# Values and output gates of the recurrent mixer, projected together from slab pairs

## What is computed

```python
proj = x @ w_in                                  # (512, 1024) @ (1024, 4096)
q, f, i, g = jnp.split(proj, 4, axis=-1)
k = (1.0 - lbf) * jax.nn.sigmoid(-ff);  q = jax.nn.silu(q);  v = i
...                                              # 8 heads of 128, chunks; state S_t = diag(f_t) S_{t-1} + k_t v_t^T
o = rms_norm(o, norm_g).reshape(B, S, HGRN_WIDTH) * jax.nn.silu(g)
return o.astype(x.dtype) @ w_out
```

## Time and profile before

| | us |
|---|---|
| median of 3 runs | 1959.66 (1959.48 to 1960.23) |
| the profiled execution | 1960.62 |
| its span, first to last instruction | 1958.9 |
| PE busy | 1933.7 (99% of the span) |
| POOL busy / DVE busy / ACT busy | 898.7 / 1103.5 / 631.9 |
| the recurrent mixer, first level products to last down product | 1320 to 1593, within the span |

### The profile page before, as it was taken

How to read it: one execution, slowest core, us unless ns; L and a number is a source line. 1 busy time by engine, 2 the same in 40 slices (tenths; PEclk the granted TensorE clock), 3 DMA queues, 4 the chain that set the end, 5 groups by cost and what they waited for, 6 DMA issues and landing times.

```text
span 1958.9 us, 26063 instructions
## 1 busy us (share of the span) xinstructions
PE 1933.7 (99%) x10793; PEld 1633.3 (83%) x10793; DVE 1103.5 (56%) x1552; ACT 631.9 (32%) x789; POOL 898.7 (46%) x596
## 2 busy tenths in 40 slices
PE   8999999999999999999999999999999999999997
PEld 8888888978779888888988888899988888888886
DVE  2755473566473765563465647365544675546555
ACT  3333232264433333322333323232233123323321
POOL 4454555543233555445445446454333345355544
PEclk9999999999999999999999999999999999999999
DMA  6232322321204233232423232322221213332321
GB/s 237 91 104 85 129 86 88 110 67 65 65 22 151 89 117 104 79 108 87 151 86 108 65 129 86 108 87 87 77 75 66 65 62 111 108 121 95 104 69 43
DMA packets 135589, 185.44 MB, mean 95 GB/s; under 512 B 3360, under 2 KB 119088, under 8 KB 135472
## 3 DMA queue, kind: packets, MB, share of 16 engines
q1 hardware_dynamic: 135312, 183.53, 28.3%
q10 hardware_dynamic: 160, 0.26, 0.1%
HBM read 181.42 MB, written 2.10 MB: 94 GB/s over the span
## 4 chain that ended last, share of the span: by engine, by line
PE 95%; DVE 3%; ACT 1%; DMA 1%; issue 0%; SPq 0%; POOL 0%; DVEq 0%; ACTq 0%
PE psum L1513 30%; PE psum L1514 29%; PE psum L1515 29%; PE psum L1823 2%; PE psum L1764 1%; PE psum L1537 1%; PE psum L1777 1%; PE psum L1796 1%; DMA raw<-in_ffn_w 1%; PE psum L1851 0%; DVE x L1112 0%; DVE arena L1223 0%; PE psum L1854 0%; PE psum L1841 0%; DVE arena L1222 0%
## 5 line engine op out<-in xcount | busy, mean ns | idle before, releaser
L693 POOL TENSOR_TENSOR w_lo<-raw,w_hi 128x512 fp32r<-128x512 f32 x524 | 848.7, 1653 | 933.1 <-ACT w_hi L756 908.6
L1513 PE MATMUL psum<-xt_hi,w_hi 128*128 128x512 f32 (+1 forms) x1824 | 675.6, 370 | 2.2 <-DVE w_lo L1383 0.9
L1514 PE MATMUL psum<-xt_lo,w_hi 128*128 128x512 f32 (+1 forms) x1824 | 670.7, 368 | 0.0
L1515 PE MATMUL psum<-xt_hi,w_lo 128*128 128x512 f32 (+1 forms) x1824 | 670.7, 368 | 0.0
L1513 PEld LDWEIGHTS psum<-xt_hi,w_hi 128*128 128x128 f32 x1824 | 343.8, 188 | 66.2 <-issue 5.5
L1515 PEld LDWEIGHTS psum<-xt_hi,w_lo 128*128 128x128 f32 x1824 | 343.9, 189 | 57.1
L1514 PEld LDWEIGHTS psum<-xt_lo,w_hi 128*128 128x128 f32 x1824 | 344.0, 189 | 55.5
L756 ACT ACTIVATE w_hi<-raw 128x2048 fp32r<-128x2048 f32 x132 | 251.8, 1911 | 341.9 <-PE psum L1515 340.0
L1072 DVE SCALAR_TENSOR_TENSOR x<-psum,x 128x512 f32<-128x512 f32 x224 | 145.4, 683 | 131.6 <-PE psum L1515 128.4
L770 ACT ACTIVATE gate<-psum 128x512 f32<-128x512 f32 x88 | 52.5, 598 | 308.9 <-PE psum L1515 308.9
L1112 DVE SCALAR_TENSOR_TENSOR x<-psum,x 128x512 f32<-128x512 f32 x124 | 83.0, 687 | 105.8 <-PE psum L1515 105.6
(11 more groups left out here) (181 smaller groups left out, 2163.1 us busy)
## 6 DMA issues: line engine op xcount, KB each, us to landing
raw<-in_ffn_w SPq DMA_DIRECT2D x115, 1024.0 KB, 5.4
raw_odd<-in_ffn_w SPq DMA_DIRECT2D x16, 1024.0 KB, 5.1
raw<-in_hgrn_w_in SPq DMA_DIRECT2D x16, 1024.0 KB, 5.4
raw<-in_attn_w_in SPq DMA_DIRECT2D x9, 1024.0 KB, 5.3
raw<-in_attn_w_out SPq DMA_DIRECT2D x4, 1024.0 KB, 5.4
raw<-in_hgrn_w_out SPq DMA_DIRECT2D x4, 1024.0 KB, 4.9
lng<-in_ln_g SPq DMA_DIRECT2D x6, 512.0 KB, 4.2
lnb<-in_ln_b SPq DMA_DIRECT2D x6, 512.0 KB, 5.2
```

Of the source, the lines that this page charges most:

```text
L693: op = pool.tensor_tensor(w_lo[:, slot_of[s], cols], raw[:, slot_of[s], cols], w_hi[:, slot_of[s], cols].bitcast(F32), ALU.subtract)
L1513: pe.matmul(out_, w[0], xs[0], start=first, stop=False)
L1514: pe.matmul(out_, w[0], xs[1], start=False, stop=False)
L1515: return pe.matmul(out_, w[1], xs[0], start=False, stop=last)
```

## The change

The v and g slabs of a group are replaced by a pair, `vg0` and `vg1`. Each holds 256 columns of v and the same 256 of g side by side (512 columns) for half of the contraction: `vg0` rows 0 to 511, `vg1` rows 512 to 1023. A quarter pair (two quarters, one block) now makes one token tile of both, 512 columns wide: its first quarter reads the slab `vg0`, its second the slab `vg1`. So both slabs of a pair are in use from the second quarter of `vg0` to the last of `vg1`.

```diff
-HGRN_PART = {"q": 0, "f": 1, "v": 2, "g": 3}
+HGRN_PART = {"q": 0, "f": 1}
+VG_HALF = {"vg0": 0, "vg1": 1}
...
-             [[("v", 0), ("g", 0), ("f", 1), ("q", 1), ("g", 1)], [("v", 1), ("down", 0), ("f", 2), ("q", 2), ("g", 2)],
-              [("v", 2), ("f", 3), ("q", 3), ("down", 1)], [("v", 3), ("g", 3), ("down", 2)]]),
+             [[("vg0", 0), ("vg1", 0), ("f", 1), ("q", 1), ("vg0", 1)],
+              [("vg1", 1), ("down", 0), ("f", 2), ("q", 2), ("vg0", 2)],
+              [("vg1", 2), ("f", 3), ("q", 3), ("down", 1)], [("vg0", 3), ("vg1", 3), ("down", 2)]]),
...
-        if step[0] == "quarter" and step[2] == 3:
+        if step[0] == "quarter" and step[2] == 3 and slabs[step[1]][0] != "vg0":
             near = [i for i in range(at + 1, min(at + 1 + reach, len(plan))) if plan[i][0] in urgent]
-            out.setdefault(near[0] if near else at, []).append(step[1] + RING)
+            freed = [step[1] - 1, step[1]] if slabs[step[1]][0] == "vg1" else [step[1]]
+            out.setdefault(near[0] if near else at, []).extend(s + RING for s in freed)
...
+            def load_vg(s, half, g):
+
+                sp.wait_ge(*raw_free[s])
+                dst = raw[:, slot_of[s], :].rearrange("p (c n) -> p c n", n=2 * GW)
+                rows = hw_in[0].rearrange("(c p) n -> p c n", p=P)[:, 4 * half:4 * half + 4, :]
+                for k in range(2):
+                    first = (2 + k) * D + g * GW
+                    sp.dma_start(dst[:, :, k * GW:(k + 1) * GW],
+                                 rows[:, :, first:first + GW]).then_inc(raw_landed[slot_of[s]], 16)
...
-                elif name == "g":
-                    op = act.activation(out_gate[:, g % 2, 2 * j:2 * j + 2, :], two_tiles, ACT.Silu)
                 else:
-                    op = act.activation(values[:, g % 2, 2 * j:2 * j + 2, :], two_tiles, ACT.Copy)
+                    t = 2 * VG_HALF[name] + j
+                    act.activation(values[:, g % 2, t, :], src[:, 0:GW], ACT.Copy)
+                    op = act.activation(out_gate[:, g % 2, t, :], src[:, GW:2 * GW], ACT.Silu)
...
+                first = s - VG_HALF.get(name, 0)
+                slot = slot_of[first + half] if name in VG_HALF else slot_of[s]
                 if quarter == 0:
                     pe.wait_ge(lo_ready, s + 1)
+                if name == "vg0" and quarter == 1:
+                    pe.wait_ge(lo_ready, s + 2)
...
+                if name in VG_HALF:
+                    t = 2 * VG_HALF[name] + j
+                    tok = slice(t * P, (t + 1) * P)
+                    for c in range(DC // 2):
+                        cols = slice(c * 2 * GW, (c + 1) * 2 * GW)
+                        c_ = half * DC // 2 + c
+                        mm = three(out_, (xt_hi[:, c_, tok], xt_lo[:, c_, tok]), (w_hi[:, slot, cols], w_lo[:, slot, cols]),
+                                   c_ == 0, c_ == DC - 1)
...
-            def outputs(g):
+            def outputs(g, blocks_needed):
+                pe.wait_ge(proj_kept, blocks_needed)
                 pe.wait_ge(states_ready, g + 1)
```

More of the change, by code:

```diff
@@ L169, in mixer_schedule, with splits @@
     return steps
-def splits(plan, urgent, reach):
+def splits(plan, slabs, urgent, reach):
     out = {}
     for at, step in enumerate(plan):
-        if step[0] == "quarter" and step[2] == 3:
+        if step[0] == "quarter" and step[2] == 3 and slabs[step[1]][0] != "vg0":
             near = [i for i in range(at + 1, min(at + 1 + reach, len(plan))) if plan[i][0] in urgent]
-            out.setdefault(near[0] if near else at, []).append(step[1] + RING)
+            freed = [step[1] - 1, step[1]] if slabs[step[1]][0] == "vg1" else [step[1]]
+            out.setdefault(near[0] if near else at, []).extend(s + RING for s in freed)
     return out
@@ L460, in build_trunk @@
                 raw_free[s], w_free[s] = last_raw.get(slot), last_w.get(slot)
-                n_loads[slot] += 1
+                n_loads[slot] += 2 if name is not None and name[0] in VG_HALF else 1
                 raw_loads[s] = 16 * n_loads[slot]
@@ L474, in build_trunk @@
                     blocks += 2
-                    last_w[slot] = proj_done, blocks
+                    last_w[slot] = proj_done, blocks + 2 * (name[0] == "vg0")
         def left_parts(name):
@@ L622, in _ @@
                             load_params(n)
+                        if name in VG_HALF:
+                            load_vg(s0 + s, VG_HALF[name], g)
+                            continue
                         if kind == "attn":
@@ L732, in _ @@
                     low(s0 + RING + 1)
-                    split_at = splits(plan, ("outputs",), 2)
+                    split_at = splits(plan, slabs, ("outputs",), 2)
                     for at, step in enumerate(plan):
@@ L967, in _ @@
                         high(s0 + s + RING)
-                    split_at = splits(plan, ("turn_out", "outputs"), 1)
+                    split_at = splits(plan, slabs, ("turn_out", "outputs"), 1)
                     for at, step in enumerate(plan):
@@ L1269, in norm_outputs @@
                 dve.wait_ge(rms_ready, g + 1)
-                dve.wait_ge(proj_kept, first_block + blocks_until("hgrn", "g", g))
+                dve.wait_ge(proj_kept, first_block + blocks_until("hgrn", "vg1", g))
                 dve.wait_ge(keys_tok_ready, 2 * g + 2)
@@ L1738, in projected @@
                 out_ = bank[j]
-                token_major = name in ("v", "g", "vb")
-                if not token_major:
+                if name in VG_HALF:
+                    t = 2 * VG_HALF[name] + j
[5 more added lines that the diff above has]
+                                   c_ == 0, c_ == DC - 1)
+                elif name != "vb":
                     for c in range(4 * half, 4 * half + 4):
@@ L1931, in _ @@
                         elif what == "updates":
-                            updates(g, first + blocks_until(kind, "v", g))
+                            updates(g, first + blocks_until(kind, "vg1", g) - 1)
                         elif what == "outputs":
-                            outputs(g)
+                            outputs(g, first + blocks_until(kind, "vg1", g))
                         elif what == "norm":
```

1 line of the change is left out of this document (removed).

## The result

The changed kernel takes **1965.09 us** (median of 8 executions, 1963.13 to 1967.9) against 1960.0 us for the kernel before (8 executions, 1959.48 to 1960.38): ratio 1.0028, 95% interval 1.0019 to 1.0036. It is slower by 5.1 us; 2.1 us were forecast, and the time lies at the upper edge of the range on record (1956.0 to 1965.2). A second set of 9 executions gave 1965.18 against 1959.93 (31 executions), the same ratio.

What follows compares the result with a forecast made beforehand. PE, busy 99% of the span, was taken to bound the kernel. Terms -4.05 - 0.4 + 0.3 + 2.15 + 3.2 + 0.9 = +2.1 us on a median of 1959.66 gave 1961.8 us, range 1956.0 to 1965.2.

Steps and rivals of the forecast that it cites:

- 8 quarters: v and g quarters of a group: 12 products of 512 columns instead of 24 of 256, 0.135 us gained each.
- level 7: Scaling ahead of this level held by back-to-back lows: +0.3 us in group 0, +3.2 us in group 2.
- level 5: Group 1: a second low in a row holds DVE's scaling, so PE waits for the add: +2.15 us.
- `low(19)` gone: Group 3: this low no longer runs between levels 6 and 7 and holds DVE's scaling: -0.4 us.
- ACT's wait: Group 3: the outputs' first product waits until ACT has kept the last vg1 block: +0.9 us.
- Group 2's walk: Ahead of group 2's level 7: four DVE instructions, each let in once per POOL piece, delay PE by 3.2 us.
- C: Rival: POOL keeps the port through a whole low, DVE gets in only at its end: +6.5 us, 1966.1; chance 0.08.
- D: Rival: PE's pace at 512 columns is no better with weights as the moving side: 1965.8 us; chance 0.04.
- A: Rival: held DVE instructions cost nothing, as PE has more slack than read: -3.6 us, 1956.1; chance 0.12.
- B: Rival: group 2's L1195 and L1197 pass freely beside a low, the rest holds: -0.4 us, 1959.3; chance 0.16.
- Part 4's cover: At the end: `low(19)` done at 1578.95, PE needs it at 1579.9; slack 0.9 us, so costed at nothing.
- part 1: v and g products: 30 of 32 quarters gain 0.135 us each from 512-column products, -4.05 us in all.

Runs made afterwards that it cites:

- apart_all: The changed kernel with slabs 6 and 15 split one slab later and slab 10 waiting for six of group 1's eight down blocks: 1956.44 us, ratio 0.9985.
- apart_g1: The changed kernel with only slab 10's split put off, waiting for six of the eight blocks of group 1's down slab: 1961.97 us, ratio 1.0012.
- again3: The changed kernel without an edit, profiled once more: 1965.91 us, mean granted clock 0.996.
- again2: The changed kernel without an edit, profiled once more: 1962.88 us, mean granted clock 0.999.

## Why the prediction was wrong, point by point

**By its own steps, at full clock.** The differences of the six points, held against the terms:

| stretch | terms on record | forecast | measured |
|---|---|---|---|
| group 0 | 8 quarters, level 7 | -0.78 | -0.36 |
| group 1 | 8 quarters, level 5 | +1.07 | +1.36 |
| group 2 | 8 quarters, level 7 | +2.12 | +2.25 |
| group 3 to its keys | 6 quarters, 2 of them without gain, `low(19)` gone | -0.94 | -0.94 |
| keys to the last down slab | 2 quarters, ACT's wait | +0.63 | +0.70 |
| sum | | +2.1 | +3.0 |

The mechanism, its places and its waits were right, and no stretch is off by more than 0.42 us, but four of the five are off the same way. Group 0: one of its quarters, that behind level 0, gains nothing, since DVE's scaling of level 1 takes as long there (3.17 us before, 3.18 after); I had looked for such quarters in group 3 only. And L1241, L1213 and L1238 beside the row of lows ahead of level 7 were held (1.26, 1.50 and 1.77 us), so the quarter ahead of the keys took 3.35 instead of 2.87. Group 1: I gave L1222, L1223 and L1225 3.5 us together (1417.78 to 1421.3); they took 3.83 (1415.81 to 1419.64), and the stop was 2.49 and not 2.15, within the range given. Group 2's walk, held instruction by held instruction, came out at 3.24 against 3.2. One slip beside the sum: the upper ends of the terms (1.0, 3.1, 3.9 and 1.4 with the -4.45 of the others) add up to 1964.6, not to 1964.9.

**The step that failed** is the sum itself: it has no term for what a stop of PE does to the products behind it. All its durations at 512 columns are from stretches with granted clock 1.00, and it took them to hold behind two new stops of 2.2 and 3.2 us as well. They don't. Of 19 executions of the changed kernel only four stand at a mean clock of 0.999, and the median carries 2 us for the others. Each fall costs 1.4 us in the execution where it can be read in rows, and 2.7 in another run. 2.1 forecast, 0.9 from the sizes of its terms and 2 from the clock make the 5.1 measured.

That 1965.09 still lies within 1956.0 to 1965.2 is luck: the range has no part for the clock, its upper end stands for longer waits than were measured, and the second set (1965.18) lies only just under it. "Slower", above 1963.6, had 0.18 for C, D and the upper end of the forecast; it came about by none of the three.

**Rivals.** A (no cost) was wrong about this kernel, but its 1956.1 is nearly what `apart_all` reaches, 1956.4: that is the change without its stops. B is out, L1211 and L1213 took 1.19 and 1.51 us. C is out too: POOL gave DVE a turn at each piece, and that the time lies near C's 1966.1 has another cause. D is out, 5.66 against 5.94.

**Part 4's cover** held. `low(19)` and `low(20)` run from 1575.47, and the first product that needs 19 started at 1581.45 with no wait for POOL. The pairs of quarters show 0.28 us for 24 products fewer, 11 to 12 ns each. (The 2.5 ns a product of the Trainium skill, "TensorE: Matmul & The Clock Gate", section "Back-to-back issue gap", would have made the gain of part 1 some 3 us smaller, an estimate; the page gives it for products by themselves, and the trace of this stream disagrees.)

## What to carry to other kernels

A new wait of the engine that bounds the kernel can cost more than its length: where a forecast adds one that the trace of before does not have, it needs a second term for the clock behind it, with a spread. When a changed kernel scatters and the old one doesn't, list time against mean granted clock per execution, see which of them the profile caught, and fill the stop with work that nobody reads. And what a change releases together (here two splits of a slab pair) is best released one by one, the second by a wait on work beside which there is slack: one wait and three splits put off turned +5.1 us into -3.4 us with the same products.

## What the runs showed of the hardware

- The granted clock can fall at a stop of TensorE of 2.5 or of 3.2 us, within it (in `apart_g1` at 1493.6, 0.7 us ahead of its end) or behind it (in `again3` at 1499.2, 1.0 us behind the end of the second), and the same program at the same place shows it in one execution and not in the next (`again2`, `again3`). It was back at 1424.2 in `again3` and at 1500.5 in `apart_g1`. In the profile of the kernel before, whose waits in the mixer are of 1.4 us at most, no stretch shows it until 1952 us, where PE has no more work.
- At 1.2 GHz a product of 512 columns takes 0.43 us from start to start, at 2.4 GHz 0.23: 1.87 times, not 2.
- Beside POOL's pieces a DVE instruction of 32 columns is held as long as one of 512 (1.25 us against 0.19 alone); copy_predicated (0.87) and scalar_tensor_tensor from PSUM (0.69) are not held.
